# Decoder layer step on 8 cores: gate r as filler of the sample recurrence, cached attention in 32-column tiles, output projection by head

## Chip, cores and metric

One Trainium2 chip, all 8 cores, no exchange between them. Each core takes 16 of the 128 sample sequences and half of one of the four prompt sequences. The metric is the device time of the slowest core in microseconds.

## What is computed

The reference is one step of a hybrid decoder layer; rmsnorm scales by the root mean square, causal_conv is a depthwise convolution with three taps.

```python
def mixer(xn, conv_prev, s0, w_in, conv_w, w_gate2, b_gate, gla_norm, w_out):
    bg, cg, vc, q, k, v, r, g1 = split(xn @ w_in)
    yc, conv_new = causal_conv(cg * vc, conv_prev, conv_w)
    logf = log_sigmoid(g1 @ w_gate2 + b_gate) / 16
    # S_t = diag(f_t) S_{t-1} + k_t^T v_t,  o_t = q_t S_t, per head (4 heads, dk 128, dv 256)
    o, s_new = gla_chunked(q, k, v, logf, s0)
    o = rmsnorm(o, gla_norm) * silu(r)
    return concat([bg * yc, o]) @ w_out, conv_new, s_new

def layer(x, ...):
    h = x + mixer(rmsnorm(x, nm), ...)
    h = h + cross_attn(rmsnorm(h, nx), mk, mv, w_xq, w_xo)   # 4 heads of 512, 256 memory tokens
    gc, ffn_new = causal_conv(hn @ w_g, prev, c_w)           # hn = rmsnorm(h, nf), 5632 channels
    return h + (silu(gc + c_b) * (hn @ w_u)) @ w_d
```

Prompt sequences compute memory keys and values from mem_prompt; samples read theirs from a cache. A final rmsnorm follows. D is 2048.

## The kernel before

Activations lie feature by token: 16 blocks of 128 features (k, or dm for outputs), NT = 1092 tokens on a core: 64 of samples (16 sequences of 4), 4 of an overlap, 1024 of the prompt. A *unit* is one block of 128 output features for all tokens: 3 chunks of 364 tokens by 16 k, 48 matmuls, into the three banks of one PSUM set, pa or pb; pc and pd are single banks. RA holds the normalized input (without the row factor rstd, which evictions multiply in), RB a second operand, RH the residual stream in f32. Cores with the second half of a prompt need the recurrent state of the first 1020 tokens, so all cores compute k and v of this prefix as well (xTp, chunks of 340).

Sched records for each operation what it reads and writes and adds the waits; every engine works its instructions in the order of the code. All matmuls carry line 154, transposes 164, ACT's activations 381 and copies 384, DVE's operations 388, 396, 400 and 572. Weights and caches come in *slabs* of up to 1 MB in bf16 (1.5 MB for the convolution) through the ring s_ws: GpSimd's queue issues them in the order of ring.add, each when ring.free has released room. The ring has 6 units of 4 KB per partition, and 8 after the sample part; most slabs take two.

The stages in order:

- x is loaded, squared and scaled; unit k of head 0 runs along.
- *Projections*: gate_main(h) makes the decay factors of head h (Exp, Ln on ACT, a scan on DVE, two Exp on ACT, two products on DVE), gate_pre(h) those of the prefix in scr[3]; k and q are units, v goes by tiles of 128 tokens in pc and pd (32 matmuls of 256 columns for two tiles, v_tiles, evicted by ACT). mem_slab makes 256 columns of the memory keys or values (32 matmuls of 256), evicts through ostg and stores. The prefix is loaded in 16 chunks (s_stgp), squared and scaled, and two products run along chunk by chunk. The memory norm is s_rstdm. r, 8 units with Silu into RB[8:16], stands at the end, in turn with four memory slabs.
- *Recurrence*: AT, khat_T (transposes of khT) and 16 sample iterations: a state is loaded to s0b (two buffers), cast to sbs, multiplied (8 matmuls of 4 columns); ds_mm gives the update, st_upd adds it in s0b, and it is stored. Then 8 chunks of 128 prompt tokens. fill(n) puts n chunks of 16 matmuls of the convolution's projections between (conv_gen, 72 in all, in pa).
- *Output projection* w_out, 16 units, then the first 4 query units of w_xq.
- *Cached attention*, 4 heads: K is a slab with the keys of 4 samples (kgroup, 68 output rows in pd, queries spread in qpad) and the scores of 256 prompt tokens, V a slab of values (128 matmuls of 4 columns), F a filler slab: query units of the next head, or in head 3 the first half of w_xo. Then the second half of w_xo.

```python
    CORD = [list('KKFKKFVVVV')] * 3 + [list('KFKFKFKFVVVV')]
```

- *Feed-forward*: fgu(fc) for 44 channel blocks (gate and up, each a unit, 14.8 us together on PE by the timeline), down(gi) in groups.
- *Last stage*: the last down product in three stretches of tokens (CLAST, 448, 448, 196), each followed by its statistic, 16 scalings by DVE and the store.

## Time and profile before

| | us |
|---|---|
| median of 3 runs | 2396.25 |
| lowest and highest of the runs | 2390.74, 2734.84 |
| profiled execution | 2393.05 |
| its span, slowest core (4) | 2392.0 |
| spans of the 8 cores | 2375.4 to 2392.0 |
| PE busy | 2079.6 (87%) |
| DVE, ACT, GpSimd busy | 824.2, 496.5, 343.3 |

The highest run is an outlier. All cores do the same work within 0.7% of each other, so core 4 speaks for all. Busy time of PE counts a matmul from start to a modelled end, at whichever clock it had.

### The profile page before, as it was taken

The numbers are of one execution on the slowest core, as the hardware profiler recorded it, in microseconds if no ns is written. First come the engines' busy times: TensorE is split into PE (matmuls) and PEld (weight loads), VectorE is DVE, ScalarE is ACT, GpSimd is POOL, SyncE is SP. The second block draws the span as 40 slices with busy tenths as digits, with TensorE's granted clock in tenths as the row PEclk, the third lists the DMA queues.
The fourth block names the chain that finished last, engine by engine and source line by source line (L and its number), as shares of the span: only waits on it lengthen the run. The fifth ranks groups of instructions, "written<-read, shape, count | busy, mean of one in ns | idle before, by whom it ended". The sixth has DMA issues, their size and how long they took to land.

```text
span 2392.0 us, 33753 instructions; the slowest of 8 cores (2375.4 to 2392.0 us)
## 1 busy us (share of the span) xinstructions
PE 2079.6 (87%) x14202; PEld 1340.1 (56%) x14202; DVE 824.2 (34%) x1183; ACT 496.5 (21%) x787; POOL 343.3 (14%) x300
## 2 busy tenths in 40 slices
PE   3858889786789999877777899999999999999985
PEld 1536667554456665554454556666666666666643
DVE  4441210123356411211232245443443433433445
ACT  4551232121122232111102410110110110100122
POOL 0000000000001133000001511210210210210234
PEclk9879999898899999988998999999999999999997
DMA  9325434755523753798956423333333333333333
GB/s 247 91 72 99 84 64 80 121 120 175 142 51 61 199 115 71 117 149 140 150 97 120 86 55 71 71 71 71 71 71 71 71 71 71 71 71 71 71 74 125
DMA packets 47574, 233.21 MB, mean 97 GB/s; under 512 B 5040, under 2 KB 15808, under 8 KB 27584
## 3 DMA queue, kind: packets, MB, share of 16 engines
q0 software_dynamic: 24080, 170.34, 40.5%
q1 hardware_dynamic: 23344, 60.71, 7.8%
q8 instruction: 114, 1.87, 0.3%
q14 instruction: 36, 0.29, 0.0%
HBM read 378.40 MB, written 22.96 MB: 168 GB/s over the span
## 4 chain that ended last, share of the span: by engine, by line
PE 77%; DMA 9%; DVE 6%; ACT 3%; issue 3%; POOL 1%; DVEq 0%; SPq 0%; ACTq 0%; POOLq 0%
PE pa L154 40%; PE pb L154 27%; PE pd L154 5%; PE pc L154 4%; DMA s_stg<-x_all 2%; DMA s_ws<-w_xq 2%; DMA s_s0b<-state_gla 1%; POOL s_accf L388 1%; DMA s_ws<-w_xo 1%; DVE s_RH L400 1%; DMA o_gla_s<-s_s0b 1%; DMA o_mv<-s_ostg 1%; DVE s_RH L388 1%; ACT s_scr L381 1%; DMA s_stgp<-x_pre 1%
## 5 line engine op out<-in xcount | busy, mean ns | idle before, releaser
L154 PE MATMUL pa<-s_RA,s_ws 128*128 128x364 bf16 x4464 | 738.0, 324 | 18.3 <-DVE s_RB L400 9.3
L154 PEld LDWEIGHTS pa<-s_RA,s_ws 128*128 128x128 bf16 x4464 | 440.1, 99 | 288.7 <-issue 40.4
L154 PE MATMUL pb<-s_RA,s_ws 128*128 128x364 bf16 x2448 | 398.3, 319 | 17.1 <-DVE s_ub L388 10.1
L154 PE MATMUL pa<-s_RB,s_ws 128*128 128x364 bf16 (+2 forms) x2016 | 330.4, 319 | 34.2 <-DVE s_RH L388 28.2
L154 PEld LDWEIGHTS pb<-s_RA,s_ws 128*128 128x128 bf16 x2448 | 236.7, 97 | 166.0 <-issue 26.9
L154 PEld LDWEIGHTS pa<-s_RB,s_ws 128*128 128x128 bf16 x2016 | 195.3, 98 | 157.2 <-issue 43.8
L154 PE MATMUL pb<-s_RB,s_ws 128*128 128x364 bf16 (+2 forms) x1632 | 270.0, 321 | 9.5 <-DMA s_ws<-w_xo 8.0
L154 PEld LDWEIGHTS pb<-s_RB,s_ws 128*128 128x128 bf16 x1632 | 159.6, 98 | 107.3 <-issue 14.8
L388 DVE TENSOR_TENSOR s_RH<-pa,s_RH 128x1092 f32<-128x1092 f32 (+2 forms) x96 | 106.1, 1105 | 216.3 <-PE pa L154 216.3
L400 DVE SCALAR_TENSOR_TENSOR s_cc<-s_gs,s_cf,s_cc 128x1027 f32<-128x1027 f32 (+3 forms) x176 | 125.1, 771 | 68.2 <-ACT s_cc L381 68.2
L388 DVE TENSOR_TENSOR s_gs<-pb,s_rstdf 128x1092 f32<-128x1092 f32 x43 | 55.7, 1295 | 265.7 <-PE pb L154 265.7
L388 DVE TENSOR_TENSOR s_RH<-pb,s_RH 128x1092 f32<-128x1092 f32 (+2 forms) x80 | 85.3, 1067 | 174.4 <-PE pb L154 174.4
L384 ACT COPY s_gtl<-s_gs 128x32 f32<-128x32 f32 x88 | 13.7, 204 | 622.8 <-DVE s_gs L388 622.8
L388 POOL TENSOR_TENSOR s_RB<-s_ub,s_cc 128x1092 bf16<-128x1092 f32 x44 | 109.4, 2486 | 30.4 <-DVE s_ub L388 18.0
L178 POOL DMA_DIRECT2D s_ws<-w_fgu x44 | 24.7, 562 | 502.0 <-PE pa L154 480.6
L381 ACT ACTIVATE s_cc<-s_cc 128x1092 f32<-128x1092 f32 x44 | 49.0, 1113 | 161.5 <-DVE s_cc L400 161.5
L388 DVE TENSOR_TENSOR s_ub<-pa,s_rstdf 128x1092 f32<-128x1092 f32 x43 | 55.7, 1295 | 28.0 <-PE pa L154 28.0
L154 PE MATMUL pd<-s_ws,s_qpad 128*68 128x256 bf16 x256 | 36.9, 307 | 28.0 <-DMA s_ws<-cache_mem_k 26.0
L381 ACT ACTIVATE s_RA<-s_RH,s_cf 128x1092 bf16<-128x1092 f32 x32 | 38.5, 1202 | 106.8 <-DVE s_RH L388 106.7
L381 ACT ACTIVATE s_cc<-s_gs,s_cf 128x1092 f32<-128x1092 f32 x44 | 57.1, 1298 | 4.1 <-DVE s_gs L396 0.4
L381 ACT ACTIVATE s_Pt<-pb,s_stat 128x256 bf16<-128x256 f32 x32 | 15.2, 474 | 184.4 <-DVE s_stat L951 182.9
L400 DVE SCALAR_TENSOR_TENSOR s_RB<-pa,s_rstdx 128x1092 bf16<-128x1092 f32 x14 | 18.1, 1294 | 94.6 <-PE pa L154 86.4
(266 smaller groups left out, 1685.8 us busy)
## 6 DMA issues: line engine op xcount, KB each, us to landing
s_ws<-w_fgu POOLq DMA_DIRECT2D x44, 1024.0 KB, 8.4
s_ws<-w_fd POOLq DMA_DIRECT2D x22, 1024.0 KB, 8.5
s_ws<-cache_mem_k POOLq DMA_DIRECT2D x16, 1024.0 KB, 14.9
s_ws<-cache_mem_v POOLq DMA_DIRECT2D x16, 1024.0 KB, 12.5
s_ws<-w_conv POOLq DMA_DIRECT2D x8, 1536.0 KB, 12.0
s_stg<-x_all SPq DMA_DIRECT2D x8, 1092.0 KB, 21.9
s_RH<-x_all SPq DMA_DIRECT2D x16, 546.0 KB, 14.7
s_ws<-w_xk POOLq DMA_DIRECT2D x8, 1024.0 KB, 10.2
```

The lines of the kernel that those rows point to most:

```text
L154: last = pe.matmul(o, lhsT=l, rhs=r, start=st, stop=sp, skip_group_check=True)
L178: self.engs[eng].dma_start(out=out, in_=in_).then_inc(self.sems[s], 16)
L381: S.op('act', lambda: act.activation(out=out, in_=in_, func=func, **kw), r=rd, w=wr)
L384: S.op('act', lambda: act.copy(out=out, in_=in_), r=[in_], w=[out])
L388: S.op(eng, lambda: e.tensor_tensor(out=out, in0=a, in1=b, op=op), r=[a, b], w=[out])
L400: S.op('dve', lambda: dve.scalar_tensor_tensor(out=out, in0=a, scalar=s, in1=b, op0=op0, op1=op1), r=rd, w=[out])
```

## The change

- The 8 units of r go from the end of the projections into conv_gen, as 24 filler chunks ahead of the convolution's 72. There is one more fill in each sample iteration, between the write of khm and its reader, and one or two elsewhere. The states have four buffers; two of them lie in rows of RB which the convolution writes later.
- The projections of heads 0 and 1 are written out: v tiles, q and k of the samples and prompt stand between the prefix's chunks, and the prefix's products follow as whole units. A gate uses a whole bank set and one Exp in place of three. The 16 memory slabs are spread: 4 after head 1, 6 in each of heads 2 and 3. Each has its own half of two ostg buffers and one store.
- Cached attention: samples go four at a time to rows 0, 32, 64 and 96 of pd, queries and probabilities spread 32 columns apart; value products have probabilities as weights and 512 columns, and are transposed back at the end of the head. Scores stand ahead of the key group, products of the prompt around the value group. w_xo is applied by head (4 k per unit): those of heads 0, 1, 2 are fillers of heads 1, 2, 3, and only the last is a pass of its own. Fillers evict by chunk.
- Sums of squares go to DVE, or in two accumulators to DVE and GpSimd. In the first feed-forward unit ub is evicted right after gs. In the last stage, a stretch's statistic comes after block 2 of the next stretch and its scalings in four parts after blocks 4, 7, 10 and 13.

```diff
-    NMEM = [3, 3, 3, 3]
...
+        for o in 'kmmqmvmmm':
...
+    CORD = ['KKFKKVVFVV', 'KFKKFKVFVVFV', 'KFKKFKVFVVFV', 'KKFKKVVFVV']
+    FORD = ['qq', 'qwqw', 'qwqw', 'ww']
...
+    def gate(h, gT, chunks, dst, n, pset):
+        w = n // 3
+        S.mms([(pset[:, ci, 0:b - a], wg2[:, h * 128:(h + 1) * 128], gT[:, a:b], True, True) for ci, (a, b) in enumerate(chunks)])
+        A_(t3(dst[:, 0:n]), v3(pset, w), AF.Exp, scale=-1.0, bias=negb[:, h:h + 1])
...
+    gate_main(0, pa)
+    pre_chunks(2)
+    iq0, wq0 = ring.get()
+    iv0, wv0 = ring.get()
+    v_main(0, wv0, 0, 4)
+    k_main(0, None, True)
+    pre_chunks(3)
+    unit(pa, lambda k: wq0[:, k, :], xa)
...
+    gate_main(1, pb)
+    pre_chunks(3)
+    v_main(0, wv0, 4, 8)
+    pre_chunks(4)
+    v_main(0, wv0, 8, 9)
+    ik1, wk1 = ring.get()
+    k_main(1, wk1)
+    pre_chunks(4)
+    q_main(1)
+    S.load('sp', memst[:, :, :], mem.rearrange("p (k m) -> p k m", k=KC))
+    stats([acc0], C3P, [pc, pd], rstdp, rstdp)
+    unit(pb, lambda k: wg1[:, k, :], xpa, 16, chunks=C3P)
+    rcols(rstdp, TILESP, 9)
+    TT(t3(g1Tp[:, :]), v3(pb, 340, 16), t3(rstdp[0:16, :]), MUL)
+    unit(pa, lambda k: wk[:, k, :], xpa, chunks=C3P)
...
+    gate_pre(0, pb)
+    TT(t3(khTp[:, :]), v3(pa, 340), t3(scr[3][:, 0:NP]), MUL)
+    gate_pre(1, pb)
+    v_pre(wv0)
+    ring.free(iv0)
+    kh_T()
+    iv1, wv1 = ring.get()
...
+    kh_T()
+    v_pre(wv1, 0, 4)
+    gate_pre(2, pa)
+    v_pre(wv1, 4, 8)
+    ring.free(iv1)
+    mem_slab()
+    S_pre(1)
+    mem_slab()
+    mem_slab()
+    mem_slab()
+    for h in (2, 3):
...
+        mem_slab()
+        kh_T()
+        mem_slab()
+        q_main(h)
...
+        for j2 in range(4):
+            i, w = ring.get()
+            for j in range(2):
+                jj = 2 * j2 + j
+                t_ = (t1, t2)[jj % 2]
+                for ci, (a, b) in enumerate(C3):
+                    S.mms([(pa[:, ci, 0:b - a], w[:, k, j * 128:(j + 1) * 128], RA[:, k, a:b], k == 0, k == KC - 1) for k in range(KC)])
+                    TT(t_[:, a:b], pa[:, ci, 0:b - a], rstd[:, a:b], MUL)
+                    if ci == 2:
+                        if j == 1:
+                            ring.free(i)
+                        A_(t_[:, :], t_[:, :], AF.Silu)
+                        TS(RB[:, 8 + jj, :], t_[:, :], glan[:, jj:jj + 1], MUL)
+                    yield
...
+        s4 = s_ % 4
+        AC(sbs[s2][:, :, :], s0b[s4][:, :, :])
         TS(khm[s2][0:68, :, :], khat[0:68, :, :], selm[0:68, s_:s_ + 1], MUL)
+        fill(1)
...
+        if 2 <= s_ < 14:
             s0_load(s_ + 2)
         fill(1 + s_ % 2)
...
+    def wo_unit(w, p, dm, j):
+        for ci, (a, b) in enumerate(C3):
+            S.mms([(pa[:, ci, 0:b - a], w[:, k, j * 128:(j + 1) * 128], RB[:, 4 * p + k, a:b], k == 0, k == 3) for k in range(4)])
+            TT(RH[:, dm, a:b], pa[:, ci, 0:b - a], RH[:, dm, a:b], ADD)
...
+        def kgroup(g):
             i, w = ring.get()
-            for s4 in range(4):
-                s_ = 4 * sg + s4
-                S.mms([(pd[0:68, 0:256], qpad[:, dc, 68 * s_:68 * s_ + 68], w[:, s4 * 4 + dc, :], s_ == 0 and dc == 0, False)
-                       for dc in range(4)])
+            S.mms([(pd[32 * s4:32 * s4 + 32, 0:256], qpad[:, dc, (4 * g + s4) * 32:(4 * g + s4 + 1) * 32], w[:, s4 * 4 + dc, :],
+                    g == 0 and dc == 0, False) for dc in range(4) for s4 in range(4)])
...
+            S.mms([(pd[32 * s4:32 * s4 + 32, :], PTs[:, mc, (4 * g + s4) * 32:(4 * g + s4 + 1) * 32], w[:, s4 * 2 + mc, :],
+                    g == 0 and mc == 0, False) for mc in range(2) for s4 in range(4)])
...
+            if dm % 3 == 2:
+                TS(RA[:, dm, :], RH[:, dm, :], gains[:, GI['ffn'], dm:dm + 1], MUL)
+            else:
+                A_(RA[:, dm, :], RH[:, dm, :], AF.Copy, scale=gains[:, GI['ffn'], dm:dm + 1])
+            if dm < 2:
+                A_(accs[dm][:, :], RH[:, dm, :], AF.Square)
+            else:
+                A_(sqf[dm % 2][:, :], RH[:, dm, :], AF.Square)
+                TT(accs[dm % 2][:, :], accs[dm % 2][:, :], sqf[dm % 2][:, :], ADD, eng='dve' if dm % 2 else 'pool')
...
+        if fc == 0:
+            TT(t3(ub[:, :]), v3(pu), t3(rstdf[:, :]), MUL)
...
+            if dm == 2 and pend is not None:
+                ys = fin(*pend)
+            if dm in (4, 7, 10, 13) and ys is not None:
+                ys((dm - 4) // 3)
+        pend = (a, b)
```

PE's order at three places. First, between the sample and prompt v tiles of head 0 and the first gate of the prefix; before, the loop over 16 chunks of the prefix begins as shown and goes on so.

```order
L154 MATMUL pc<-s_ws,s_RA 128x256 x32
L154 MATMUL pd<-s_ws,s_RA 128x256 x32
L154 MATMUL pc<-s_ws,s_RA 128x256 x16
L154 MATMUL pa<-s_xTp,s_wg_65 16x340 x3
L154 MATMUL pb<-s_xTp,s_ws 128x340 x3
L154 MATMUL pa<-s_xTp,s_wg_65 16x340 x3
L154 MATMUL pb<-s_xTp,s_ws 128x340 x3
```

Now:

```order
L154 MATMUL pa<-s_RA,s_ws 128x364 x48
L154 MATMUL pb<-s_g1T,s_wg_55 128x364 x3
L154 MATMUL pc<-s_ws,s_RA 128x256 x32
L154 MATMUL pd<-s_ws,s_RA 128x256 x32
L154 MATMUL pc<-s_ws,s_RA 128x256 x16
L154 MATMUL pa<-s_RA,s_ws 128x364 x96
L154 MATMUL pc<-s_acc_94,s_onesf 128x340
L154 MATMUL pd<-s_acc_94,s_onesf 128x340
L154 MATMUL pc<-s_acc_94,s_onesf 128x340
L154 MATMUL pb<-s_xTp,s_wg_65 16x340 x48
L154 MATMUL pd<-s_onesf,s_rstdp 128x1 x7
```

The prefix loop of small pairs has gone behind the tiles and units of heads 0 and 1, and stands as one block of 48 (wg1) after the statistic.

Second, the first sample iterations of the recurrence; s_sbs is the cast state, s_khm the masked keys, rows with pa and x16, x32 are fillers. Before:

```order
L154 MATMUL pc<-s_qt,s_sbs_4046 128x4 x8
L154 MATMUL pb<-s_vt,s_khm_4048 128x256 x2
L154 MATMUL pd<-s_vt,s_khm_4048 128x256 x2
L154 MATMUL pa<-s_RA,s_ws 128x364 x16
L154 MATMUL pc<-s_qt,s_sbs_4047 128x4 x8
L154 MATMUL pb<-s_vt,s_khm_4049 128x256 x2
L154 MATMUL pd<-s_vt,s_khm_4049 128x256 x2
L154 MATMUL pa<-s_RA,s_ws 128x364 x32
```

Now:

```order
L154 MATMUL pa<-s_RA,s_ws 128x364 x16
L154 MATMUL pc<-s_qt,s_sbs_3503 128x4 x8
L154 MATMUL pb<-s_vt,s_khm_3505 128x256 x2
L154 MATMUL pd<-s_vt,s_khm_3505 128x256 x2
L154 MATMUL pa<-s_RA,s_ws 128x364 x32
L154 MATMUL pc<-s_qt,s_sbs_3504 128x4 x8
L154 MATMUL pb<-s_vt,s_khm_3506 128x256 x2
L154 MATMUL pd<-s_vt,s_khm_3506 128x256 x2
L154 MATMUL pa<-s_RA,s_ws 128x364 x48
```

Each iteration has one filler chunk more: 2 or 3 of them lie between iterations instead of 1 or 2.

Third, cached head 1; s_qpad are the spread queries, s_PTs the spread probabilities. Before:

```order
L154 MATMUL pd<-s_ws,s_qpad 68x256 x16
L154 MATMUL pb<-s_mkT,s_RB 128x256 x8
L154 MATMUL pd<-s_ws,s_qpad 68x256 x16
L154 MATMUL pb<-s_mkT,s_RB 128x256 x8
L164 MATMUL pc<-s_identb,s_Pt 128x128 x4
L154 MATMUL pa<-s_RA,s_ws 128x364 x96
L154 MATMUL pd<-s_ws,s_qpad 68x256 x16
L154 MATMUL pb<-s_mkT,s_RB 128x256 x8
L164 MATMUL pc<-s_identb,s_Pt 128x128 x4
L154 MATMUL pd<-s_ws,s_qpad 68x256 x16
L154 MATMUL pb<-s_mkT,s_RB 128x256 x8
L164 MATMUL pc<-s_identb,s_Pt 128x128 x4
```

Now, from the first scores on:

```order
L154 MATMUL pb<-s_mkT,s_RB 128x256 x8
L154 MATMUL pd<-s_ws,s_qpad 32x256 x16
L154 MATMUL pa<-s_RA,s_ws 128x364 x96
L154 MATMUL pb<-s_mkT,s_RB 128x256 x8
L154 MATMUL pd<-s_ws,s_qpad 32x256 x16
L164 MATMUL pc<-s_identb,s_Pt 128x128 x4
L154 MATMUL pb<-s_mkT,s_RB 128x256 x8
L154 MATMUL pd<-s_ws,s_qpad 32x256 x16
L164 MATMUL pc<-s_identb,s_Pt 128x128 x4
L154 MATMUL pa<-s_RB,s_ws 128x364 x96
L154 MATMUL pb<-s_mkT,s_RB 128x256 x8
L154 MATMUL pd<-s_ws,s_qpad 32x256 x16
```

Output rows went from 68 to 32, and a filler of w_xo (pa<-s_RB) came in.

## Rows read from the trace of the kernel before

**Rows 1.** Windows of core 4: stretch, us, busy PE, PEld, DVE, ACT, POOL, clock, DMA share.

```profile
61.30:278.90 217.60, 164.37 (x1129) 115.60 (x1128) 73.46 (x85) 86.46 (x146) 5.81 (x11) 0.84 0.38 84
278.90:513.90 235.00, 209.19 (x1577) 155.65 (x1575) 32.82 (x31) 51.16 (x102) 9.49 (x18) 0.95 0.55 100
513.90:651.30 137.40, 92.85 (x634) 56.37 (x633) 54.99 (x130) 21.83 (x25) 6.62 (x5) 0.83 0.54 150
651.30:804.00 152.70, 140.11 (x1037) 91.85 (x1038) 89.33 (x171) 41.23 (x64) 16.53 (x12) 0.94 0.34 65
804.00:964.70 160.70, 152.50 (x967) 94.14 (x966) 30.41 (x28) 40.05 (x42) 49.61 (x28) 0.99 0.55 124
964.70:1281.60 316.90, 243.87 (x2040) 163.69 (x2040) 70.93 (x120) 40.94 (x123) 21.77 (x41) 0.92 0.78 132
1281.60:1353.00 71.40, 61.72 (x385) 37.91 (x385) 21.35 (x17) 33.38 (x31) 34.47 (x17) 0.91 0.58 103
2284.70:2392.00 107.30, 71.07 (x390) 40.92 (x390) 51.38 (x100) 29.14 (x56) 45.99 (x47) 0.83 0.32 94
```

**Rows 2.** Timeline of PE in the projections of the last head.

```profile
365.61 7.08 PE L154 MATMUL pb<-s_xTp,s_ws 128*128 128x340 bf16 x48
372.52 7.56 PE L154 MATMUL pa<-s_RA,s_ws 128*128 128x364 bf16 x48
379.93 3.65 PE L154 MATMUL pd<-s_ws,s_RA 128*68 128x256 bf16 x32
383.42 3.66 PE L154 MATMUL pc<-s_ws,s_RA 128*128 128x256 bf16 x32
```

**Rows 3.** Waits of PE over the whole run: us in total, times, longest.

```profile
PE pd L154 <- DMA s_ws<-cache_mem_k: 26.0, 5, 7.9
PE pc L154 <- ACT s_sbs L384: 24.1, 7, 7.6
PE pc L154 <- DVE s_rstdm L388: 20.0, 1, 20.0
...
PE pd L164 <- DVE s_khT L396: 17.5, 5, 5.5
...
PE pb L154 <- DVE s_ub L388: 10.1, 1, 10.1
```

**Rows 4.** Timeline of ACT in the gate of head 0.

```profile
69.75 0.56 ACT L381 ACTIVATE s_scr<-pc,s_cf 128x364 f32<-128x364 f32 x1
...
76.01 2.10 ACT L381 ACTIVATE s_scr<-s_scr 128x1092 f32<-128x1092 f32 x2
```

**Rows 5.** Timeline of POOL, the issue of the first slab of cached head 1.

```profile
1017.88 0.53 POOL L178 DMA_DIRECT2D s_ws<-cache_mem_k  x1 [6.67 <-PE pd L154]
```

**Rows 6.** Timeline of PE in cached heads 0 and 1.

```profile
1014.42 2.13 PE L154 MATMUL pb<-s_PT,s_mvb 128*128 128x512 bf16 x8
...
1028.20 3.57 PE L154 MATMUL pd<-s_ws,s_qpad 128*68 128x256 bf16 x16 [7.46 <-DMA s_ws<-cache_mem_k]
...
1041.83 9.24 PE L154 MATMUL pa<-s_RA,s_ws 128*128 128x364 bf16 x48 [2.34 <-DMA s_ws<-w_xq]
1052.62 7.56 PE L154 MATMUL pa<-s_RA,s_ws 128*128 128x364 bf16 x48 [1.55 <-DVE s_RB L400]
1060.02 1.91 PE L154 MATMUL pd<-s_ws,s_qpad 128*68 128x256 bf16 x16
1061.76 1.04 PE L154 MATMUL pb<-s_mkT,s_RB 128*128 128x256 bf16 x8
```

**Rows 7.** Groups by form in the second output pass: count, busy us, mean ns.

```profile
L388 DVE TENSOR_TENSOR s_RH<-pb,s_RH 128x1092 f32<-128x1092 f32 x8 | 10.4, 1294 | 33.9 <-PE pb L154 33.9
```

**Rows 8.** Timeline of DVE in the last stage.

```profile
2323.54 9.62 DVE L400 SCALAR_TENSOR_TENSOR s_RH<-s_RH,s_cf,s_rl 128x448 f32<-128x448 f32 x16 [6.72 <-ACT s_rl L381]
...
2340.34 0.62 DVE L388 TENSOR_TENSOR s_RH<-pb,s_RH 128x448 f32<-128x448 f32 x1 [0.89 <-PE pb L154]
...
2383.27 5.42 DVE L400 SCALAR_TENSOR_TENSOR s_RH<-s_RH,s_cf,s_rl 128x196 f32<-128x196 f32 x16 [5.16 <-ACT s_rl L381]
```

517 lines of the change are left out of this document (261 added, 256 removed).

## Prediction

> **What bounds the kernel now.** I read the windows first [rows 1], then the waits of TensorE (PE) [rows 3], then the timeline of PE at the places that these name. PE is the longest busy engine in every stretch, and the long feed-forward part between 1380.3 and 2284.7 us is solid PE work that the change leaves as it is. So the question is how far the other stretches are from solid PE work. The unit prices are start to start: 48 matmuls of 364 columns take 7.41 us, 48 of 340 take 6.91, 32 of 256 take 3.49 (0.109 each) [rows 2].
>
> Projections, 61.3 to 513.9 us, 452.6 us. By count the work is 1600 matmuls of 256 columns (v 576 and 512, memory slabs 512): 174.5 us; 15 units of 48 at 7.41: 111; five at 6.91: 34.5; gates, transposes, statistics, some 22. That is 342, so 110 us are waits and half clock. The largest wait is 20.0 us for the memory norm [rows 3], and the granted clock of the first stretch is 0.84, which mixes its two levels of 1.2 and 2.4 GHz [rows 1].
>
> Recurrence with convolution as filler, 513.9 to 804 us, 290.1 us. Work: 72 filler chunks of 2.47 (a third of 7.41) are 178; 100 matmuls of 256 columns are 11, the some 400 smaller ones at half that price 22: 211. The other 79 are waits for the cast state (24.1), for khT (17.5) and others, and the clock, 0.83 in its first and 0.94 in its second part [rows 1, 3].
>
> Cached attention, 964.7 to 1281.6, then the second output pass to 1353. DMA is busy for 0.78 of the first [rows 1]. At its worst the slabs set the pace: the first slab of head 1 is issued at 1017.88 [rows 5], lands for 1028.20, and the third for 1041.83 [rows 6]: 10 us for the first, 6.8 for each that follows. 42 slabs in 317 us are 7.5 each.
>
> **The change, part by part.**
>
> 1. *Gate r leaves the projections.* 8 units of 7.41 are 59 us off that stretch. It still has 283 us of PE work. What of the 110 us stays? The PE order now does v, q and k while the prefix's chunks are prepared, so the 20.0 us and the waits in the prefix loop go. In their place come waits behind in-order ACT. A gate takes ACT from 69.75 to 78.11, 8.4 us, most of it waiting for the scan on DVE [rows 4], and evictions of v tiles now stand behind gates and prefix squares. I laid these orders side by side: v tile 8 waits for the evictions behind gate 1 and three prefix chunks, about 8 us; the prefix v of head 0 waits for the second gate_pre, whose scratch the first must release, about 7; statistics and transposes of the memory norm 6; restarts at the lower clock 8. Three memory slabs in a row take PE 10.5 us and DMA 20, so the ring adds about 3 us in each of three places, and the first r slab 4. The sum is about 42 to 47. Kept: 47 of 110. The stretch takes 283 + 47 = 330 and saves 123, of which 59 are the moved work. Bounds: if ACT and DVE, 138 and 106 us busy in the two stretches [rows 1], hide everything, 10 are kept (saving 160); if the order only reshuffles, 80 are kept (saving 90).
>
> 2. *r becomes filler.* 24 chunks more: 96 x 2.47 + 33 = 270 us. The sample iterations have 40 chunks instead of 24, so each has 2.5 x 2.47 + 0.7 = 6.9 us of PE work. Before, the 16 iterations and their start took 137.4 us [rows 1], 8.6 each, for they waited for state loads through two buffers. Four buffers and 6.9 us of work cover a store and a load in turn; a filler chunk now stands between the khm write and its reader; the first transpose has two chunks ahead of it. I keep no state wait, 5 us in the sample part and 15 in the chunked part, where DVE order is as it was: 290 us, as long as before. Where that cover fails, this costs up to 59.
>
> 3. *w_out and the first query units*, 160.7 us [rows 1]: the same matmuls. The accumulation goes from GpSimd to DVE, which is busy 30 of 161 us. qpad's memset goes ahead of the slabs' issues on GpSimd's queue, where it waits for the last reads of the recurrence; four w_out slabs are loaded then, so nothing is late. Nothing.
>
> 4. *Cached attention.* One key group is 16 matmuls with 68 output rows, 1.74 us (1060.02 to 1061.76), a query filler 2 x 7.41 and 1.55 of wait for the single bank set [rows 6]. Now the tiles are 32 wide, the fillers evict chunk by chunk (DVE needs 1294 / 3 = 431 ns and a fixed part, against 0.62 us of PE for a chunk of 4 matmuls [rows 7]), the w_o product moves in by head, and fillers stand among the value slabs. What four 32-column tiles cost no row shows. The upper bound is one after another at the price of their columns: 1.74 for a key group as now, and for a value group 8 matmuls of 512 columns, at 2.13 / 8 = 0.27 [rows 6] 2.1 us, for 128 tiny ones now. The lower bound is four at once, a quarter of that. I take the upper. Work on PE: 12 filler slabs of 14.8 are 178; 16 key groups with scores and transposes of 2.85 are 46; 16 value slabs with products of 3.1 are 50; head ends 8: 282 us. The slabs: 44, three landed at the start, 41 x 6.8 = 279. The two are equal, and a ring of four slabs couples them badly at head ends; walking through with 6.8 per slab gives 288, and I add 5 for each of three starts of heads (the chain of sample softmax, transposes, the queries' spreading): 303. With tiles at once PE has 30 less, but DMA stays: 284 instead of 288.
>
> By the Trainium skill, TensorEngine Tiling (Array Packing), "Theoretical Speedup", tiles of 32 columns run up to four at a time; by its "Key Properties" a change of tiling mode drains TensorE, which speaks against so many small groups. No run here shows either yet. The first would take 4 us off the sum above; the second is the rival E.
>
> 5. *Last output pass.* 16 units of 12 matmuls x 0.154: 29.6 on PE, but per unit DVE adds (1.29), scales a third and accumulates half: 2.2, so 35, and 5 for the last slabs: 40. Together 343 against 388.3: saving 45. Bounds: PE and DMA in perfect overlap 282 + 35 = 317 (saving 71); heads as slow per slab as now, 44 x 7.5 = 330, + 45 (saving 13).
>
> 6. *First feed-forward unit.* PE waits 10.1 for ub, which was evicted after the taps [rows 3]; now right after gs: 5 sooner, and 1 of clock: 6.
>
> 7. *Tail*, 107.3 us. After the first and second stretch of columns, 16 scalings of 9.62 us [rows 8] stood between PE and its banks, after a statistic. They now go in four parts among the next stretch's work. DVE there has 9.6 + 16 x 0.62 + 7 x 0.6 (an accumulation, estimated at the price of such an addition) = 23.7, PE 128 x 448 columns at 7.41 / (48 x 364) = 24.3: even. 4.3 for the last product before it, 27, 25, then 17 for the short stretch (DVE), 2.5 statistic, 5.4 scaling [rows 8], 3.3 to the end as now (2392.0 less 2388.7): 85. Saving 22, within 12 to 27.
>
> **Sum.** 123 + 0 + 0 + 45 + 6 + 22 = 196. The profiled execution took 2393.05 us, its span 2392.0. So 2197; the median of the three runs is 3 us higher: **2200 us**.
>
> **The rivals.**
>
> B. *ACT's order eats the projections' gain.* Evictions behind two chained gates hold PE banks, PE idles, its clock falls to 1.2 GHz. For: the 8.4 us of one gate [rows 4], seven gates left to pass. Against: ACT is busy under half of the time. At the bound of 80 kept us: 33 more, 2233.
>
> C. *The slabs stay the bound and the attention gives only its lower bound.* For: DMA at 0.78, seldom a slab ahead; against: fillers now give each head 59 us in which loads run. 13 instead of 45: 2232. With B: 2265.
>
> D. *Better overlap than I allow*: 20 kept us in the projections rather than 47, 300 for heads: 2200 - 27 - 10 = 2163.
>
> F. *r isn't free*: DVE, busy 55 and 89 us of the recurrence's 290 [rows 1] and given 24 evictions, 8 gains and sparse waits more, becomes the bound there, and half of the 59 comes back: 2230.
>
> E. *The slower side.* Each 32-column matmul pays a drain rather than its columns. There are 256 + 16 + 128 + 8 = 408. To end over 2393 + 48 they must cost (193 + 48) / 408 = 0.59 us each beyond 0.11 to 0.27. The nearest rows give 0.11 for 68 output rows at full clock and 3.57 / 16 = 0.22 at the lower [rows 6]. Nothing in the profile nears 0.59; 2445.
>
> **How the numbers follow.** Forecast (2180 to 2218) 0.45; B, C or F alone (2218 to 2245) 0.24; two of them (to 2275) 0.10; D (2140 to 2180) 0.17; in between 2345 and 2440 0.02; E 0.01; other 0.01. The range 2150 to 2262 leaves out about 0.15. 2% is 48 us, about what a measurement of this kernel tells from no change. Faster by more: 0.96; within: 0.025; slower: 0.015.
>
> **What would show it.** In the changed profile: the first AT product near 391 us; w_out starting near 681; no waits for sbs of over 1 us; heads of 55, 85, 85 and 60 us with DMA over 0.85; a key group's 16 matmuls in 1.7 us (one by one) or 0.5 (at once); the feed-forward part at 14.8 us a unit as before; a tail of 85. I am wrong if the projections end after 425, if the recurrence takes over 310, or if a group of small tiles takes over 4 us.

## Result, and the profile after

The changed kernel takes 2295.9 us at the median of four runs (2290.5 to 2304.3), beside 2393.5 for the kernel before on the same chip: ratio 0.961, 95% interval 0.955 to 0.966. It is faster by about 98 us where the prediction had 193, and lies above its range. Some executions ran slower on the four cores of one die or on all, with a lower granted clock; ratios leave them out, and where every execution was such (e13 to e18) there is no ratio, and the numbers are read from cores of the profile that did not.

The profiled execution spans 2289.4 us on its slowest core, 102.6 less than before. The windows of that core, cut where PE passes from one stage to the next (columns as in [rows 1]):

```profile
core 2: us, PE busy (x) PEld busy (x) DVE busy (x) ACT busy (x) POOL busy (x), PEclk, DMA share, GB/s
62.00:413.80 351.80, 299.57 (x2318) 233.33 (x2318) 98.21 (x118) 118.84 (x212) 13.79 (x26) 0.94 0.52 102
413.80:577.20 163.40, 140.16 (x957) 86.87 (x958) 73.75 (x166) 32.81 (x38) 7.67 (x7) 0.88 0.66 163
577.20:742.60 165.40, 148.96 (x1098) 97.87 (x1097) 92.36 (x166) 39.68 (x59) 16.55 (x12) 0.94 0.31 61
742.60:903.80 161.20, 153.46 (x968) 94.50 (x966) 49.14 (x42) 39.95 (x42) 11.31 (x14) 0.98 0.54 122
903.80:1198.70 294.90, 252.68 (x1841) 145.15 (x1842) 130.35 (x272) 46.38 (x157) 23.32 (x44) 0.94 0.88 153
1198.70:1251.40 52.70, 35.59 (x193) 19.88 (x194) 34.62 (x27) 27.17 (x26) 16.43 (x8) 0.90 0.40 81
1251.40:1276.70 25.30, 20.39 (x109) 12.12 (x110) 3.93 (x4) 4.94 (x9) 2.57 (x3) 0.91 0.47 84
1276.70:2182.60 905.90, 905.90 (x5856) 566.91 (x5856) 370.96 (x472) 120.15 (x175) 141.45 (x103) 1.00 0.40 71
2182.60:2289.40 106.80, 70.98 (x396) 41.16 (x396) 66.74 (x118) 28.04 (x56) 24.14 (x23) 0.82 0.30 94
```

Against the stages before and the terms of the prediction (us; the first begins 0.7 later than before):

| stage | before | predicted | after | saving predicted | saving found |
|---|---|---|---|---|---|
| projections | 452.6 | 330 | 351.8 | 123 | 101 |
| recurrence | 290.1 | 290 | 328.8 | 0 | -39 |
| w_out, first queries | 160.7 | 160.7 | 161.2 | 0 | 0 |
| heads and last output pass | 388.3 | 343 | 347.6 | 45 | 41 |
| first feed-forward unit | 27.3 | 21 | 25.3 | 6 | 2 |
| feed-forward | 904.4 | 904.4 | 905.9 | 0 | -1.5 |
| tail | 107.3 | 85 | 106.8 | 22 | 0 |

Three terms hold nearly all of the miss: the recurrence (39), the projections (22) and the tail (22). The waits of PE in the changed kernel, largest first (total, times, longest); the first is the load ahead of all work:

```profile
PE pa L154 <- DMA s_wg<-w_g: 22.7, 1, 22.7
PE pc L164 <- ACT s_PT L384: 18.3, 8, 3.9
PE pc L154 <- DVE s_acce L388: 15.7, 2, 9.1
PE pb L154 <- DVE s_RH L388: 15.2, 6, 3.4
PE pc L154 <- ACT s_sbs L384: 14.4, 6, 6.9
...
PE pa L154 <- DVE s_RH L388: 11.3, 7, 4.1
PE pd L164 <- DVE s_khT L396: 9.5, 2, 5.8
PE pb L154 <- DVE s_khm L396: 8.9, 2, 6.1
```

Beside [rows 3]: the 26.0 for cache_mem_k, the 20.0 for rstdm and the 10.1 for ub are gone. The wait for sbs fell only from 24.1 to 14.4, that for khT from 17.5 to 9.5. New are 15.7 for acce, an accumulator that the change brought into the tail, and 18.3 for PT, where transposes of the heads want the one bank pc again.

**Recurrence.** The longest waits there come with these rows: the queue of SyncE ahead of the first state load, and VectorE and GpSimd around 563.7, where PE waits for khm until 566.25.

```profile
413.77 0.42 PE L154 MATMUL pc<-s_qt,s_kt 128*68 128x68 bf16 x4 [3.75 <-DVE s_mvb L396]
434.05 0.35 PE L154 MATMUL pc<-s_qt,s_sbs 128*128 128x4 bf16 x8 [6.87 <-ACT s_sbs L384]
566.25 0.59 PE L154 MATMUL pb<-s_vt,s_khm 68*128 68x256 bf16 x2 [6.15 <-DVE s_khm L396]
398.86 14.94 SPq L178 DMA_DIRECT2D o_mv<-s_ostg  x3
426.25 0.34 SPq L178 DMA_DIRECT2D s_pcc<-cache_conv  x1
426.64 2.16 SPq L178 DMA_DIRECT2D s_s0b<-state_gla  x4
559.77 2.84 DVE L400 SCALAR_TENSOR_TENSOR s_t<-s_t,s_cf,s_t 128x1027 f32<-128x1027 f32 x4 [1.49 <-ACT s_t L381]
562.71 0.60 DVE L400 SCALAR_TENSOR_TENSOR s_t<-s_pcc,s_cf,s_t 128x16 f32<-128x16 f32 x2
563.24 0.53 DVE L388 TENSOR_TENSOR s_t<-pa,s_rstd 128x364 f32<-128x364 f32 x1
563.68 2.42 DVE L396 TENSOR_SCALAR s_khm<-s_khat,s_cf 68x512 bf16<-68x512 bf16 x1
563.48 2.47 POOL L388 TENSOR_TENSOR s_RB<-s_t,s_t 128x1092 bf16<-128x1092 f32 x1 [4.70 <-DVE s_t L400]
```

Two things are to be seen. The load of s_pcc waits 12.4 us for a store from ostg1, whose address it shares in the kernel, and the four state loads stand behind it in SyncE's queue. And khm stands behind a conv unit's taps and an eviction on VectorE; once begun it takes 2.42 us, where its median is 0.34, and ends within 0.15 us of GpSimd's product.

**Heads.** A key group, 16 matmuls, took 1.74 from start to start [rows 6]; here a group of 32 output rows takes 0.56 (from 982.80 to 983.36; its row reads 0.62, to the modelled end). Below it a value group of 8 where the granted clock is low (0.50 from 934.60 to 935.70), and one at full clock:

```profile
961.34 0.62 PE L154 MATMUL pd<-s_ws,s_qpad 128*32 128x256 bf16 x16 [0.68 <-ACT s_qpad L384]
...
934.67 1.04 PE L154 MATMUL pd<-s_ws,s_PTs 128*32 128x512 bf16 x8
...
955.38 0.62 PE L154 MATMUL pd<-s_ws,s_PTs 128*32 128x512 bf16 x8
```

**Tail.** The second stretch of 448 columns on VectorE, and PE's two waits for acce:

```profile
2230.33 1.24 DVE L388 TENSOR_TENSOR s_acce<-s_acce,s_sq 128x448 f32<-128x448 f32 x1 [0.77 <-ACT s_sq L381]
2231.49 2.46 DVE L400 SCALAR_TENSOR_TENSOR s_RH<-s_RH,s_cf,s_rstdf 128x448 f32<-128x448 f32 x4
2233.88 0.61 DVE L388 TENSOR_TENSOR s_RH<-pa,s_RH 128x448 f32<-128x448 f32 x1
2234.41 0.61 DVE L388 TENSOR_TENSOR s_RH<-pb,s_RH 128x448 f32<-128x448 f32 x1
2235.80 1.24 DVE L388 TENSOR_TENSOR s_acce<-s_acce,s_sq 128x448 f32<-128x448 f32 x1 [0.78 <-ACT s_sq L381]
...
2251.53 1.83 PE L154 MATMUL pc<-s_accf,s_onesf 128*128 128x448 f32 x2 [6.63 <-DVE s_acce L388]
2277.87 0.99 PE L154 MATMUL pc<-s_accf,s_onesf 128*128 128x196 f32 x2 [9.05 <-DVE s_acce L388]
```

In these rows VectorE has no gaps but the 0.77 before each sum: it adds a block, must wait for ScalarE's square of that same block, and only then goes on.

### The profile page after: what moved, and what is told of

The parts are those of the page before. It is cut to its first block, busy times and chain, and to the rows that moved or that the text cites. A ratio compares the mean times of both kernels' runs of the same rounds, so it can differ in the third digit from the quotient of the medians.

```text
span 2289.4 us, 33324 instructions; the slowest of 8 cores (2266.9 to 2289.4 us)
## 1 busy us (share of the span) xinstructions
PE 2051.2 (90%) x13822; PEld 1305.2 (57%) x13822; DVE 946.1 (41%) x1410; ACT 484.2 (21%) x786; POOL 263.4 (12%) x254
## 4 chain that ended last, share of the span: by engine, by line
PE 78%; DMA 9%; DVE 5%; ACT 4%; issue 3%; POOL 0%; SPq 0%; DVEq 0%; ACTq 0%; POOLq 0%
PE pa L154 43%; PE pb L154 27%; PE pd L154 4%; PE pc L154 4%; DMA s_stg<-x_all 2%; DMA s_s0b<-state_gla 1%; DVE s_RH L400 1%; DMA o_mv<-s_ostg 1%; DMA s_ws<-w_xo 1%; DMA s_ws<-w_xq 1%; DVE s_RH L388 1%; ACT s_scr L381 1%; DMA s_ws<-w_xk 1%; DVE s_scr L579 1%; DVE s_t L400 1%
## 5 line engine op out<-in xcount | busy, mean ns | idle before, releaser
L154 PE MATMUL pa<-s_RA,s_ws 128*128 128x364 bf16 x4656 | 762.0, 323 | 14.0 <-DVE s_RH L388 5.3
L154 PEld LDWEIGHTS pa<-s_RA,s_ws 128*128 128x128 bf16 x4656 | 457.6, 99 | 293.5 <-issue 31.1
L154 PE MATMUL pb<-s_RA,s_ws 128*128 128x364 bf16 x2256 | 371.8, 321 | 12.3 <-DVE s_gs L396 4.9
L154 PE MATMUL pa<-s_RB,s_ws 128*128 128x364 bf16 (+2 forms) x2112 | 347.8, 321 | 16.4 <-DMA s_ws<-w_xo 6.1
L154 PEld LDWEIGHTS pb<-s_RA,s_ws 128*128 128x128 bf16 x2256 | 219.3, 98 | 152.6 <-issue 25.2
L154 PE MATMUL pb<-s_RB,s_ws 128*128 128x364 bf16 (+2 forms) x1536 | 255.4, 321 | 17.8 <-DVE s_RH L388 15.2
L388 DVE TENSOR_TENSOR s_RH<-pa,s_RH 128x364 f32<-128x364 f32 (+3 forms) x224 | 161.8, 725 | 132.2 <-PE pa L154 122.2
L388 DVE TENSOR_TENSOR s_t<-pa,s_rstd 128x364 f32<-128x364 f32 x72 | 38.2, 534 | 76.7 <-PE pa L154 70.9
L400 DVE SCALAR_TENSOR_TENSOR s_RB<-pa,s_rstdx 128x364 bf16<-128x364 f32 (+1 forms) x38 | 21.9, 577 | 85.0 <-PE pa L154 85.0
L154 PE MATMUL pc<-s_ws,s_RA 128*128 128x256 bf16 (+1 forms) x288 | 39.3, 303 | 12.2 <-ACT s_vt L381 6.1
```

Of the source, the lines that this page charges most:

```text
L154: last = pe.matmul(o, lhsT=l, rhs=r, start=st, stop=sp, skip_group_check=True)
L388: S.op(eng, lambda: e.tensor_tensor(out=out, in0=a, in1=b, op=op), r=[a, b], w=[out])
L400: S.op('dve', lambda: dve.scalar_tensor_tensor(out=out, in0=a, scalar=s, in1=b, op0=op0, op1=op1), r=rd, w=[out])
```

## The experiments

Each is the changed kernel with one edit, unless it says otherwise. Times of a stage are from PE's timeline, its first instruction to the next stage's first, on the slowest core where one number stands, and as a median of the cores where it says so; by that median of eight the recurrence takes 285.4 before and 323.0 after. The slowest core is not the same one from run to run, and the cores of one profile differ by 10 us and more in the recurrence, so the medians are the safer comparison.

**e1, gate r out of the filler.**

```
-    filler: 24 chunks of r, then 72 of conv
+    8 units of r ahead of the recurrence, filler: 72 chunks of conv
```

> The changed kernel with gate r taken out of the filler again: its 8 units of 48 matmuls stand in one block between the last memory slab and the recurrence, and the recurrence gets the filler pattern of the kernel before (72 chunks). Everything else is as in the changed kernel (2295.9 us, recurrence 328.8 us in its profile). The block costs 8 x 7.41 = 59 us wherever it hides nothing. Theory 1 (r as filler gained only a part, because the waits of the recurrence come from the state loads and from VectorE's order, which more filler does not shorten): the recurrence falls from 329 to about 290, the whole is some 20 us slower than the changed kernel, 2316. Theory 2 (my prediction: the filler is free, it only takes the place of idle time): the recurrence stays near 329 and the whole is 59 slower, 2355. Theory 3 (r was not free at all): the recurrence falls by 59 to 270 and the whole stays at 2296.

Measured: 2289.3 us, ratio 0.958 (0.955 to 0.960): not slower. On the slowest core the recurrence takes 262.1 and the stretch ahead of it 64 more. By the median of eight cores the recurrence falls by 61.4, from 323.0 to 261.6, and the stretch ahead grows by 57.7. So r as filler gains nothing over a plain block of r; its 24 chunks are 59.3 us of work. My theories 1 and 2 fall; theory 3 holds. Up to 5 us of the 61.4 have a reason beside the filler: SyncE issues the first state loads while PE works on the block, and PE's first wait for them falls from 6.2 to 1.3 in the median. Without it the 24 chunks would still cost 56, so r as filler hides 3 of its 59 us at most.

The waits of PE in e1's recurrence:

```profile
PE pb L154 <- DVE s_khm L396: 16.5, 16, 2.7
PE pd L164 <- DVE s_khT L396: 12.4, 4, 5.5
PE pc L154 <- ACT s_sbs L384: 7.7, 4, 3.1
```

All waits there sum to 37 us in the median of the eight cores, and to 37 in the changed kernel too. The chunk between khm's write and its reader does take away the short waits for khm (16 in e1, 2 in the changed kernel). But the two that are left are long, the waits for the cast state are more, and 4.8 us for Am and 2.2 for the filler's own buffer t are new.

**e2, state loads ahead of the conv cache.**

```
-    load pcc; load s0b 0 to 3
+    load s0b 0 to 3; load pcc
```

> The changed kernel with one load moved: the load of the conv cache (s_pcc), which stands in SyncE's queue ahead of the first four state loads and waits 12.4 us there until the store from ostg1 has landed (the two share an address), now stands behind them. Theory 1 (the first wait for sbs, 6.9 us at 434.05, is this queue order): the first state load is issued near 414 instead of 426.6, the 6.9 us go and the stores and loads behind have more lead, so the 4.5 us at 512 go too; 7 to 12 us off the recurrence, 2286. Theory 2 (a state load takes 6 to 13 us beside the weight slabs, and the loads in series set the pace whenever they begin): the first wait goes, others of the same sum come later; under 3 us gained.

Measured: ratio 0.958 (0.955 to 0.962); the recurrence's median of eight cores goes from 323.0 to 320.0, and PE's first wait for sbs from 6.2 to 4.0. This is nearest to theory 2: the four loads, issued at once, still land too late for the first reader. Single cores differ by more than these 3 us.

**e3, conv product on VectorE.**

```
-    TT(RB[:, jj, :], t2[:, :], t3b[:, :], MUL, eng='pool')
+    TT(RB[:, jj, :], t2[:, :], t3b[:, :], MUL)
```

> The changed kernel with the last product of each conv unit (1092 columns, 2.47 us on GpSimd, eight times in the recurrence) on VectorE instead. In the profile VectorE's khm takes 2.42 us instead of 0.34 and its four khT 2.97 instead of 0.73 when they begin beside that product, and end with it; then PE waits 6.2, 5.8, 4.8 and 3.7 us. Theory 1 (these VectorE instructions stand still until GpSimd is done): khm and khT go back to 0.34 and 0.73 everywhere, VectorE does the product in about 1.3 us instead, and each of the waits is some 1 us shorter; the recurrence gains 4 to 10 us. Theory 2 (the waits are only VectorE's order, taps ahead of khT): VectorE has 1.3 us more in front of the same readers, each wait grows by 1.3, and the recurrence loses 5 to 10 us.

Measured: 2285.7, ratio 0.957 (0.954 to 0.959), which overlaps the changed kernel's interval. First the tile khT, its durations (min, median, max in ns) in the changed kernel, then here:

```profile
L396 DVE TENSOR_SCALAR s_khT<-s_kt,s_expL x36: 217/248/2478, 414.8 to 699.0; 128x128 bf16<-128x128 bf16 x32, 128x4 bf16<-128x4 bf16 x4
```

```profile
L396 DVE TENSOR_SCALAR s_khT<-s_kt,s_expL x36: 217/247/251, 414.0 to 695.3; 128x128 bf16<-128x128 bf16 x32, 128x4 bf16<-128x4 bf16 x4
```

The longest falls from 2478 to 251 ns, that of khm from 2417 to 343. So VectorE did stand still for GpSimd. But PE's waits for khm and khT stay, 9.6 and 9.2 us for 8.9 and 9.5: VectorE now has the product itself in front of the same readers. The recurrence's median falls by 1.1 us. The mechanism of theory 1 is shown; the 4 to 10 us that it promised are not found.

**e8, head 3's gates behind the v tiles of head 2.**

```
     q_main(2)
-    gate_main(3); mem_slab(); gate_pre(3)
+    mem_slab()
     v_main(2); v_pre
+    gate_main(3); gate_pre(3)
```

> The changed kernel with the main and prefix gates of head 3, both of head 3's gates that is, moved from around the third memory slab of head 2 to behind head 2's prefix v tiles. Theory 1 (the 5.8 us that PE waits for ostg at 280.97, and further waits of the evictions behind the gates, are the price of the chain scan, two exponentials, two products ahead of the slab's eviction on VectorE and ScalarE): the stretch up to the recurrence gets 6 to 10 us shorter. Theory 2 (the gates must be paid for somewhere, at the v tiles or ahead of k of head 3): the wait moves there, and the stretch stays within 3 us of its 351.8.

Measured: ratio 0.962 (0.957 to 0.968). The 5.8 us at 280.97 are gone, and a longer wait stands where the gates stand now:

```profile
322.76 1.87 PE L154 MATMUL pd<-s_vp,s_khp 128*128 128x256 bf16 x8 [11.78 <-DVE s_ostg L388]
```

The stretch ahead of the recurrence is 7 longer on the slowest core and 2.9 by the median of eight. Theory 2: the wait moves, and nothing is gained.

**e4, e5, e7: three ways for the sums of squares.** e4: tail, all sums on GpSimd. e5: last pass and tail, each sum behind the next block's addition. e7: tail, squares as bf16, summed by TensorE:

```
 e4: -eng='pool' if dm % 2 == 0 else 'dve'   +eng='pool'
 e5: -add block dm; square dm; sum dm        +add block dm; sum dm - 1; square dm
 e7:
+    bk += onesb.T @ sq(dm - 2)      # one matmul per block, into one bank per stretch
-    acce[:, a:b] += sq(dm)          # on VectorE for odd dm, GpSimd for even
```

> The changed kernel; in the tail alone the sums of squares of the odd blocks are added on GpSimd as those of the even blocks are, not on VectorE. The tail takes 106.8 us in the changed kernel, where I had predicted 85. Theory 1 (VectorE is the bound of the tail: 16 additions of 0.62, four groups of scalings of 2.5 to 3.3 and eight sums of 0.6 to 1.2, each behind 0.77 of waiting for ScalarE's square, are 34 us a stretch of 448 columns against 24 on PE): without the sums VectorE has 21 to 24, and the tail takes 88 to 92. Theory 2 (it is the statistic behind the last square, in whatever engine): GpSimd has 16 sums of 1.13, its last one is no earlier, and the tail stays within 4 us of 107. Theory 3 (GpSimd's sums hold up VectorE's operations on SBUF, as the 3.3 us for a group of scalings beside a sum show): twice as many of them eat half of the gain, 98.

> The changed kernel; in the last output pass (52.7 us, predicted 40) and in the tail (106.8, predicted 85) each sum of squares is issued behind the residual addition of the following block instead of behind its own. Engines and amounts are as they were. Theory 1 (VectorE, in order, stands idle for the square that ScalarE forms of what VectorE has just written: 0.77 us each in the tail, 1.3 to 3.3 each in the pass, and PE then waits for its banks): the pass falls to 38 to 42 and the tail by 8 x (0.77 + 0.77 + 0.57) = 17 at most to about 92. Theory 2 (the engines are full, by VectorE's slower operations beside GpSimd): the idle time turns into nothing, pass and tail each change by under 4 us.

> The changed kernel; in the tail ScalarE writes the squares as bf16 and TensorE sums them over blocks and partitions at once, 16 matmuls with a matrix of ones into one bank per stretch, each two blocks late. No engine adds squares any more, and the f32 statistic matmuls go. PE gets 16 x 0.19 = 3 us more a stretch of 448. By theory 1 (VectorE bound) VectorE has 9.9 + 9.9 = 20 a stretch and PE 27: the tail takes 4.3 + 27 + 27 + 17 to 20 for the short stretch with its scalings, + 2.5 + 5.4 + 3.3 = 87 to 90. By theory 2 (a serial chain of statistic and scaling sets it) over 100.

| kernel | whole, us | ratio (95%) | last pass | tail |
|---|---|---|---|---|
| changed | 2295.9 | 0.961 (0.955 to 0.966) | 52.7 | 106.8 |
| e4 | 2289.6 | 0.956 (0.954 to 0.958) | 54.4 | 109.3 |
| e5 | 2276.6 | 0.950 (0.948 to 0.952) | 43.2 | 99.6 |
| e7 | 2276.1 | 0.950 (0.948 to 0.952) | 52.7 | 88.6 |

e7 took what theory 1 said. It takes the sums off VectorE and off GpSimd as well, and with them the f32 matmuls of the statistic. e4 takes the same sums off VectorE alone and gains little: the tail's median of eight cores falls from 108.2 to 105.7. Its rows show why, VectorE first, then GpSimd:

```profile
2249.33 0.61 DVE L388 TENSOR_TENSOR s_RH<-pa,s_RH 128x448 f32<-128x448 f32 x1
2249.86 5.10 DVE L400 SCALAR_TENSOR_TENSOR s_RH<-s_RH,s_cf,s_rstdf 128x448 f32<-128x448 f32 x4
...
2249.81 1.13 POOL L388 TENSOR_TENSOR s_accf<-s_accf,s_sq 128x448 f32<-128x448 f32 x1 [2.54 <-ACT s_sq L381]
2250.90 1.51 POOL L388 TENSOR_TENSOR s_acce<-s_acce,s_sq 128x448 f32<-128x448 f32 x1
```

Four scalings take 5.10 us beside GpSimd's sums, 2.46 alone, and the sums 1.51 for 1.13; the addition from a PSUM bank keeps its 0.61. Theory 3 was right in kind and too mild. So VectorE's own sums and its stalls beside GpSimd's sums together bound the tail; it shortens much only when both go. The Trainium skill, SBUF — State Buffer, "SBUF: two separate sides", has a port pair that VectorE and GpSimd share as an exclusive lock and not as a split of the bandwidth, for VectorE's fast modes and, against a GpSimd operation that reads SBUF, for its operations with two SBUF inputs. The three rows (khm 2.42 for 0.34, the scalings 5.10 for 2.46, the addition from PSUM unchanged) agree.

In e5 the pass falls by 9.5 and the tail by 7, half of what theory 1 said there: the 0.77 us gaps shrink to 0.24 or nothing, but VectorE still has the sums, and its groups of scalings take 3.0 to 3.3 beside GpSimd's.

**e6, e10: the small tiles.** e6 goes through one tile after the other. e10 puts all on one tile; it leaves out three quarters of the sample rows of scores and values, while the number and size of the matmuls stay.

```
 e6:  -for dc in range(4) for s4 in range(4)   +for s4 in range(4) for dc in range(4)
 e10: -(pd[32 * s4:32 * s4 + 32, 0:256], ...   +(pd[0:32, 0:256], ...
```

> The changed kernel with the order of the small tiles turned round: the matmuls of a key group (16) and of a value group (8) run through one 32-column tile after the other instead of going round the four tiles. Same matmuls. In the changed kernel a key group's 16 take 0.55 us from start to start and a value group's 8 take 0.98, where one matmul of 256 columns takes 0.11 and one of 512 takes 0.22. Theory 1 (neighbours in the order run side by side only when they are for different tiles): 16 in turn take 1.74, 8 take 1.8 to 2.1; PE gets 16 x 1.2 + 16 x 1.0 = 35 us more, of which the waits in the heads (42 us of 295) take up a part, so the heads last 10 to 35 us longer. Theory 2 (the tiles overlap whatever the order): 0.55 and 0.98 stay, and nothing changes.

> The changed kernel with all small matmuls of the cached attention (key and value groups) put on the first 32-column tile of the array instead of on four; their number and size are the same. What is left out: three quarters of the sample rows of scores and values are not formed, all are summed into one set of 32 rows. In e6 the order of the tiles made no difference (key group 0.55 to 0.58 us, value group 0.56 to 0.98). Theory 1 (four tiles run side by side whatever the order, and only a shared tile makes them serial): a key group takes 16 x 0.109 = 1.74 us, a value group 8 x 0.22 = 1.8; 35 us more for PE in the four heads. If the slabs are the bound, as my prediction had it (DMA is busy 0.88 of the heads), the heads grow by only 4 to 10 us from 295; if PE's own chain is, by 30 to 35. Theory 2 (a matmul with 32 output rows is fast by itself): the groups stay at 0.55 and 0.98 and nothing changes.

Measured: e6 2294.1, ratio 0.958 (0.956 to 0.960); e10 ratio 0.962 (0.955 to 0.970). A key group in e6, then in e10:

```profile
962.89 0.65 PE L154 MATMUL pd<-s_ws,s_qpad 128*32 128x256 bf16 x16 [0.68 <-ACT s_qpad L384]
```

```profile
965.84 1.91 PE L154 MATMUL pd<-s_ws,s_qpad 128*32 128x256 bf16 x16 [0.68 <-ACT s_qpad L384]
```

In e6 it stays at 0.65, so the order does not matter. On one tile it takes 1.91, and PE is busy 287.5 us of the heads instead of 252.7. For these 35 us the heads grow by 11, from 294.9 to 305.8 (by 14 from the median of eight, 291.7), while DMA's share goes from 0.88 to 0.85. So the tiles run side by side, and most of what they save PE was already hidden behind the slabs.

**e9, e13: the four state buffers.** e9 is the changed kernel with two; e13 is the kernel before with four.

> The changed kernel with two buffers for the sample states instead of four, and each load issued right behind its iteration's store, as in the kernel before. With e1 this makes a square of recurrences: two buffers and 72 filler chunks 290.1 us (before), four and 72 262.1 (e1), four and 96 328.8 (changed), two and 96 this one. The 24 chunks of r are 59.3 us of PE work. Theory 1 (the four buffers and the r filler pay for the same idle time: either takes away the waits for the state loads, and the second finds none left): 96 chunks with two buffers take 328 to 338, so r as filler would have gained some 15 to 25 us with two buffers and gains nothing with four. Theory 2 (the filler covers nothing in any case, since its slabs' loads slow the state loads by as much): 290 + 59 = 349 or more.

> The kernel before with one part of the change alone: four buffers for the sample states, loaded two sequences ahead. Theory 1 (from e1 and e9: the four buffers by themselves take the waits for the state loads away, 28 us, and leave none for r as filler): the recurrence goes from 290.1 to about 262, the whole to 28 us under the kernel before, ratio 0.988. Theory 2 (they only help together with other parts of the change, as the earlier start or the spread memory slabs): under 8 us.

Measured: e9 ratio 0.965 (0.959 to 0.971); e13 has none. The recurrence, median over the eight cores (e13's lie between 269.4 and 277.4, and its two dies agree, 271.9 and 272.7):

| | 72 filler chunks | 96 filler chunks (r in) |
|---|---|---|
| two buffers | 285.4 (before) | 335.8 (e9) |
| four buffers | 272.3 (e13) | 323.0 (changed) |

The buffers give 13.1 in the first column and 12.9 in the second, whatever the filler. Each of these pairs differs in the buffers alone, so this price is clean. It is half of the 28 that theory 1 had for e13. For e9 theory 1 had the right number (328 to 338) and a wrong reason: it had the buffers and the filler pay for the same idle time, but the buffers give as much without r in the filler as with it.

The rows of the square, 50.4 and 50.7 apart, are not the price of the 24 chunks: the left column belongs to the kernel before, the right one to the changed kernel, with everything else that differs ahead of and in the recurrence. Inside the changed kernel e1 gives that price, 61.4 (56 without the first wait). The difference from 50.7, 10.7, is what e13 (272.3) and e1 (261.6) differ by, both with four buffers and 72 chunks. Half of it lies in the start: the first cast state is read 12.9 us into the recurrence in e13 and 7.4 in e1, behind the same work. In e13, as in the kernel before, the first transposes wait 4.93 for khT; in the changed kernel and in e1 two filler chunks stand ahead of them, and this wait is gone:

```profile
518.18 0.61 PE L164 MATMUL pd<-s_identb,s_khT 128*68 128x128 bf16 x4 [4.93 <-DVE s_khT L396]
```

**e11, khm and khT one iteration ahead.**

```
+        TS(khm[1 - s2], khat, selm[s_ + 1])     # then the four state updates of s_
+        kh_ts(ci + 1)                           # then the squares and update of ci
```

> The changed kernel with the two small scalings of the recurrence, khm and khT, issued one iteration ahead: khm of the next sequence before the state updates of this one, khT of the next chunk before the squares and the state update. VectorE has the same work in another order. Theory 1 (8.9 us of waits for khm, 9.5 for khT and parts of those for Am come from VectorE's order: these scalings stand behind the taps, or behind updates that wait): 12 to 18 us of the 328.8 go. Theory 2 (PE only meets the next link of VectorE's chain: the state update, the casts, the sums through p2): the waits carry other names, and under 5 us go.

Measured: ratio 0.952 (0.946 to 0.959). Recurrence 308.1 on the slowest core, median 306.4: 16.6 less. Theory 1: the waits for khm and khT (8.9 and 9.5) are gone, and two of 1.2 and 1.1 for the updates stand there. Those for Am grow from 4.8 to 7.4, and one of 3.6 for the squares is new; all waits together fall from 37 to 27 us in the median:

```profile
L154 PE MATMUL pb<-s_vt,s_khm 68*128 68x256 bf16 x34 | 6.6, 277 | 1.2 <-DVE s_s0b L400 1.2
L154 PE MATMUL pc<-s_qt,s_sbs 128*128 128x4 bf16 x128 | 5.5, 164 | 11.7 <-ACT s_sbs L384 11.7
L164 PE MATMUL pd<-s_identb,s_khT 128*128 128x128 bf16 x32 | 3.3, 230 | 1.1 <-DVE s_Sst L400 1.1
```

**e12, r between the last memory slabs** (based on e1).

> e1 with the four slabs of gate r not in one block but one behind each of the last memory slabs of head 3 (and one at the end), so that their units of 14.8 us stand where PE waits for memory slabs, for S_pre's operands and for the mvb evictions: 1.3, 2.3 and 3.8 us, with the lower clock behind them. Theory 1 (the r units are useful as cover where the projections wait, not in the recurrence): 8 to 12 us less than e1's 2289, 2279. Theory 2 (nothing is waited for longer than the unit that covers it moves it): within 3 us of e1.

Measured: 2280.7, ratio 0.953 (0.947 to 0.959). The stretch ahead of the recurrence is 4.4 shorter than in e1 by the median of eight cores, the recurrence as long (261.3 to 261.6). Between the two theories.

**e14 to e18, the parts together.** e14: e2, e3, e5's pass, e7 and e11 on the changed kernel. e15: the same with r as in e12 and 72 chunks of filler. e16: e15 with the product on GpSimd. e17 and e18 repeat e14 and e15.

> The changed kernel with what held, r still as filler: states loaded ahead of the conv cache (e2: 3 us), khm and khT one iteration ahead (e11: 20.7), the conv product on VectorE (e3: 4.6 alone, some 2 of it after e11), the sums of the last pass one block later (e5: 9.5), the sums of the tail on PE (e7: 18.2). If the parts add up: 53 us less than 2296, 2243, recurrence 303, tail 88.6. If the recurrence's parts cover each other, recurrence 308 and 2248.

> As e14, but gate r in units between the last memory slabs as in e12, and the recurrence with 72 filler chunks. In e1 and e12 PE waits 16.5 us for khm, 12.5 for khT and 8 for sbs there. Theory 1 (VectorE's order was what made the waits, so it is worth at least as much with less filler): the recurrence falls from 261 to about 237, the whole to 2281 - 24 - 5 - 9.5 - 18 = 2224, 20 less than e14. Theory 2 (with 1.5 chunks a sequence, the chain khm, products, four updates of 0.4 us each is itself as long as the filler; only more filler covers it): the recurrence stays over 250, and e15 is no better than e14.

> e15 with the conv product back on GpSimd. Theory 1 (VectorE's scalings stand still beside GpSimd's 2.5 us, and each time something PE needs is among them): 3 to 8 us slower than e15. Theory 2 (with khm and khT issued ahead nothing that PE needs soon runs beside the product, and VectorE is glad of the 1.3 us): equal, or faster by up to 5.

> The kernel of e14 once more, beside e18, since that set gave no ratio to the kernel before. From the undisturbed die of e14 (longest span 2243.1 us, recurrence 307 to 311, pass 43.2, tail 88.5): 2243 to 2250, ratio 0.939. If the parts had not added up it would stay over 2260.

> The kernel of e15 once more. Its undisturbed die has 2242.3 at the longest, recurrence 253.5 (96 chunks less 24: e14's 308 less 59.3 would be 249), projections 51 to 54 us longer than e14's. Theory 1 (r between the slabs covers waits there that it does not cover in the recurrence): 5 to 10 us faster than e17. Theory 2 (equal to the filler, each place has waits of its own): within 3 us of e17.

None has a ratio. Cores 0 to 3 of the profiles read as follows (those of e17 ran at a clock of 0.817 to 0.835 and are left out):

| | longest span | recurrence, median of 4 | pass | tail, slowest core |
|---|---|---|---|---|
| changed | 2289.4 | 323.2 | 52.7 | 106.8 |
| e14 | 2243.1 | 306.6 | 43.2 | 88.5 |
| e15 | 2242.3 | 253.6 | 43.6 | 89.7 |
| e16 | 2249.4 | 257.5 | 43.2 | 88.6 |
| e18 | 2241.1 | 252.1 | 43.2 | 88.5 |

The span is some 46 us under the changed kernel's, 2% of it, where the parts had promised 53. Where nothing was changed, from the end of the last pass to the first product of 448 columns, e14's core takes 935.0 us and the changed kernel's 935.5, so the cores can be compared. e14 and e15 are equal: with r in either place, projections and recurrence together take 653 to 663 us (e14) and 653 to 661 (e15) on these cores. The order edit, with e2 and e3 beside it, is worth less with 72 chunks (261.3 to 253.6, e12 to e15) than with 96 (323.0 to 306.4 by itself): what PE waits for there is the cast state and the state update, not the order. e16 is 7 us longer than e15 in span and 4 in the recurrence, on the side of its theory 1, but on four cores of one execution.

## Why the prediction was half right

**Right.** The direction, and the step on the cached attention: 41 of 45 us. Within it the heads took 294.9 where I had 303, and the pass 52.7 where I had 40, so two errors cancelled. The lower price for the tiles was the true one (0.56 from start to start against the 1.74 I took), and my statement that it would be worth little, since the slabs pace the heads, held in kind: e10 puts it at 11 to 14 us, I had said 4. At the price that I took, one after another, e10 has PE busy 287.5 us and the heads at 305.8, close to my 282 and 303. Nothing for w_out and the feed-forward part held.

**Wrong, and the largest: step 2, "r becomes filler", 290 us.** It said that the work grows by 59 and the waits and the clock fall by as much, from 79 to 20. Of the reasons given, four buffers are worth 13 us (e13, e9), and the two chunks ahead of the first transposes take away a wait of 4.9. The longer cover per iteration is worth 3 us at most: with r in the filler or out of it PE waits 37 us in all, and taking the 24 chunks out takes 61.4 off, of which up to 5 have another reason (e1). The filler between khm and its reader ended the short waits for khm, but not where khm itself was late: it and khT stand behind a conv unit's taps in VectorE's order, and moving them ahead is worth 16.6 us (e11). What I called no state wait is 14.4 us. The stretch has 53 us of waits and lower clock by the median of eight cores (323 less my 270 of work), not 20, and my sign of being wrong, over 310 us, came; so did waits for sbs of over 1 us, which I had excluded. The sum also took its 79 us from the waits for the cast state and khT and never priced those for khm, 12.2 us in eleven waits before. Rival F came nearest, "VectorE becomes the bound", with half of the 59 coming back and 2230; by e1 nearly all of the 59 came back, and not because VectorE is full (166 of 329 us busy) but, for the 16.6 us of e11, because of what stands first in its queue. e3 shows that a full exchange of 20 us of GpSimd's work changes 1 us.

**Wrong by size: step 1, the projections, 47 us kept.** The places were right: v tile 8 waits 6.1 (I had 8), the prefix v of head 0 5.3 (7), the memory norm 4.0 (6), two memory slabs 2.8 and 2.3 (3 each). I had not walked through heads 2 and 3: 5.8 for ostg behind head 3's gate, 2.1 and 2.3 for slabs, 3.8 for mvb. All of PE's waits in the stretch sum to 52 (351.8 less 299.6 busy), and the lower clock takes the other 17: 69 kept of 110 where I had 47 (my listed terms sum to 42). It is the step between the forecast and rival B (80). Ordering alone saved 41, not 63. e8 tried to get the largest unforeseen wait back and gained nothing: the gate's chain has to be passed somewhere.

**Wrong: step 7, the tail, 85 us.** The sum for VectorE (23.7 a stretch) left out three things that its rows show: the 0.77 us before each sum, for the square of the block just written; the sums and scalings that stretch beside GpSimd's (0.62 to 1.24, 2.46 to 3.33); and that the second stretch's scalings fall into the short third one, for which I took 17 us of additions alone. With the sums on TensorE the tail takes 88.6 (e7), close to my 85. So the deferred scaling can be worth about what I had said, and the sums ate it.

**Step 5, last pass, 40 us:** 52.7, from the same coupling: a sum waits for ScalarE behind the addition it belongs to. One block later it takes 43.2 (e5). **Step 6**, 6 us: 2 found; PE now waits 4.9 for gs instead of 10.1 for ub.

**Slips in the sums.** Rival D takes 10 us off for heads of 300; against 303 that is 3, so it stood at 2170. The signs for the heads, 55, 85, 85 and 60, add up to 285 and not to 303; measured from head to head they are 56, 88, 85 and 66. Neither changes the argument.

**Still open.** The other half of the 10.7 us between e13 and e1, what sets the waits for the cast state that stay with four buffers (14.4 us), and the ratio of the combined kernels.

## What to carry to other kernels

Work used as filler is only free where the wait it covers has nothing to do with the filler's own tail: here each conv unit brought taps and evictions to VectorE, and the small operations that PE needed next stood behind them. To price filler, compare it with the same work in a plain block of the same kernel (e1), not with another kernel. Before moving work under a wait, write down the other engines' order at that place, and move the small operation that PE needs ahead of the filler's. An operation that reads what another engine makes of one's own last result should stand one block later in an in-order engine's queue, and the sum over partitions and blocks cost least on TensorE here (e7).

## What the runs showed of the hardware

VectorE and GpSimd hold each other up on SBUF operands: 0.34 us became 2.42, four scalings 5.10 instead of 2.46, and GpSimd's sum 1.51 instead of 1.13, while additions with one operand in PSUM kept their 0.61. Moving sums from VectorE to GpSimd gave 2.5 us by the median of the cores (e4), where taking them off both gave 18 (e7), and the f32 statistic went with them.

Matmuls with 32 output columns of the array on four different tiles ran side by side in either order of issue, 16 in 0.62 to 0.65 us against 1.91 on one tile (e6, e10). One theory for e6 had been that only neighbours on different tiles overlap. Going from full-width matmuls to these tiles cost nothing that the rows show: the value group above begins at 934.67, and the product ahead, 1.06 us from 933.68, ends at 934.74. My rival E of 0.59 us a matmul does not appear. Nor does the drain that the Trainium skill, TensorEngine Tiling (Array Packing), "Key Properties", names for a change of tiling mode.
